# First attention of a two-part transformer block: plain F32 scores for both components in the two halves of the array, with seven weight chunks between the heads

## What is computed

```python
qkv = hn @ w_qkv                                  # hn: 512 x 1024, w_qkv: 1024 x 3072
q, k = apply_rope(q), apply_rope(k)               # (S, 8 heads, 2 components, 64)
s = einsum('bqhcd,bkhcd->bhcqk', q_blk, k) * scale
s = where(causal_mask, s, -inf)
p = softmax(s, axis=-1)
a = p[:, :, 0] - lam * p[:, :, 1]                 # the two components are combined
o = einsum('bhqk,bkhe->bqhe', a, v)
o = rms_norm(o, subln_g) * (1 - lambda_init)
h = h + o @ w_o
```

## Time and profile before

| what | value |
|---|---|
| median of 3 runs | 1865.9 us (1862.34 to 1867.95) |
| the profiled execution | 1863.19 us, with a span of 1861.4 us |
| PE busy | 1832.0 us, 98% of the span |
| DVE, ACT, POOL busy | 908.1, 614.0, 526.7 us |
| mean granted TensorE clock | 0.996 of full |

### The profile page before, as it was taken

The page is one execution under the profiler, slowest core; times in us unless marked ns, Lnnn a source line. Parts: engine busy times, 40 slices in busy tenths (PEclk is TensorE's granted clock), DMA queues, the critical chain, the costliest instruction groups (busy, mean ns, idle before and its releaser), DMA issues.

```text
span 1861.4 us, 22776 instructions
## 1 busy us (share of the span) xinstructions
PE 1832.0 (98%) x8694; PEld 1498.8 (81%) x8694; DVE 908.1 (49%) x1146; ACT 614.0 (33%) x888; POOL 526.7 (28%) x340
## 2 busy tenths in 40 slices
PE   9999999999999999999999999999999999999998
PEld 7897788888888876788888888777777888888876
DVE  7746753333335765453333335498655432333366
ACT  4236622122223335422222124233435232222352
POOL 1311355142325430153223245332112220210222
PEclk9999999999999999999999999999999999999999
DMA  5525322322322224225222222311112232232231
GB/s 181 163 91 117 101 93 95 106 93 90 107 96 90 91 98 136 93 90 125 100 104 90 95 105 91 121 68 68 46 60 94 89 109 90 90 113 91 90 113 68
DMA packets 40558, 183.94 MB, mean 99 GB/s; under 512 B 5512, under 2 KB 12200, under 8 KB 21416
## 3 DMA queue, kind: packets, MB, share of 16 engines
q1 hardware_dynamic: 38224, 179.26, 28.5%
q10 hardware_dynamic: 2264, 3.72, 1.0%
HBM read 161.99 MB, written 3.67 MB: 89 GB/s over the span
## 4 chain that ended last, share of the span: by engine, by line
PE 88%; DVE 6%; issue 2%; ACT 1%; POOL 1%; DMA 1%; SPq 0%; DVEq 0%; ACTq 0%; POOLq 0%
PE ps L496 23%; PE ps L497 23%; PE ps L498 23%; PE ps L546 4%; PE ps L535 4%; PE ps L536 4%; PE ps L705 1%; PE ps L896 1%; PE ps L914 1%; PE ps L819 1%; PE ps L809 1%; DVE probs L1612 1%; DVE wlo L1465 1%; DVE negmin L1591 1%; DVE idx_score L1879 1%
## 5 line engine op out<-in xcount | busy, mean ns | idle before, releaser
L1465 DVE TENSOR_TENSOR wlo<-raw,whi 128x2048 fp32r<-128x2048 f32 x138 | 341.7, 2476 | 325.8 <-ACT whi L1019 323.2
L1019 ACT ACTIVATE whi<-raw 128x2048 fp32r<-128x2048 f32 x147 | 280.6, 1909 | 373.0 <-PE ps L498 263.7
L496 PE MATMUL ps<-xb,whi 128*128 128x512 f32 x992 | 388.0, 391 | 3.2 <-ACT idx_relu L1294 1.3
L498 PE MATMUL ps<-xb,wlo 128*128 128x512 f32 x992 | 386.1, 389 | 0.0
L497 PE MATMUL ps<-xb,whi 128*128 128x512 f32 x992 | 386.0, 389 | 0.0
L496 PE MATMUL ps<-xa_hi,whi 128*128 128x512 f32 x788 | 307.6, 390 | 0.8 <-DVE wlo L1465 0.7
L498 PE MATMUL ps<-xa_hi,wlo 128*128 128x512 f32 x788 | 306.6, 389 | 0.0
L497 PE MATMUL ps<-xa_lo,whi 128*128 128x512 f32 x788 | 306.6, 389 | 0.0
L496 PEld LDWEIGHTS ps<-xb,whi 128*128 128x128 f32 x992 | 186.3, 188 | 44.1 <-issue 4.7
L498 PEld LDWEIGHTS ps<-xb,wlo 128*128 128x128 f32 x992 | 186.2, 188 | 39.2
L497 PEld LDWEIGHTS ps<-xb,whi 128*128 128x128 f32 x992 | 186.3, 188 | 38.2 <-issue 0.2
(11 more groups left out here) (324 smaller groups left out, 2524.0 us busy)
## 6 DMA issues: line engine op xcount, KB each, us to landing
raw<-wst SPq DMA_DIRECT2D x149, 1024.0 KB, 4.8
stage<-qk_split SPq DMA_DIRECT2D x64, 128.0 KB, 2.4
h<-xT ACTq DMA_DIRECT2D x4, 512.0 KB, 7.9
stage_k_lo<-qk_split SPq DMA_DIRECT2D x32, 64.0 KB, 2.0
mla_qn<-q_nope SPq DMA_DIRECT2D x8, 256.0 KB, 2.7
mla_v<-v_tok SPq DMA_DIRECT2D x8, 256.0 KB, 2.7
outT<-h SPq DMA_DIRECT2D x8, 256.0 KB, 2.0
bias_scratch<-bias_rows ACTq DMA_DIRECT2D x1, 1536.0 KB
```

What stands on the lines that cost most here:

```text
L496: pe.matmul(out, lhs_hi, rhs_hi, start=first, stop=False)
L498: return pe.matmul(out, lhs_lo, rhs_hi, start=False, stop=last)
L1019: act.activation(whi[slot][:, :], raw[slot][:, :], ACT.Copy).then_inc(whi_done, 1)
L1465: dve.tensor_tensor(wlo[slot][:, :], raw[slot][:, :], whi[slot][:, :].bitcast(F32), ALU.subtract).then_inc(wlo_done, 1)
```

## The change

The stages `qk`, `v` and `diff` become one stage `qkv` of 12 chunks in the order q, k, v for each pair of heads. Chunks 0 to 4 run ahead, and chunks 5 to 11 run one in each of the steps -1 to 5. The fp32r split of q and k is gone, with `qk_split`, `stage_k_lo` and the memsets that cleared its other half. `stage` now holds plain F32, component 0 in rows 0 to 63 and component 1 in rows 64 to 127, with 4 DMAs for each head. For each query block PE makes one F32 product over 64 rows for each component, one after the other into two banks, and then the two mask products. A single pair of banks takes the scores: banks 0 and 1 up to head 3 (`SWAP`), banks 2 and 3 from head 4, and for the last head the two pairs in turn. The other pair takes the chunk's tiles. The weighted sum of head n now stands in step n (before: n+1), and `turn` of head n-1 behind it (before: n-3). The loops over heads are written out.

```diff
-            def diff_scores(par, half, comp, first=False):
-                pe.wait_ge(stage_full[par][comp], 96 * (half + 1))
...
-                    pe.matmul(b[:, 0:wide], stage[par][:, comp, 0, q], stage[par][:, comp, 1, 0:wide], start=True, stop=False)
-                    pe.matmul(b[:, 0:wide], stage[par][:, comp, 0, q], stage_k_lo[par][comp][:, 0:wide],
-                              start=False, stop=False)
-                    mask_later(b[:, q]).then_inc(tile_done, 1)
+            def diff_scores(n, i):
+                banks = score_banks(n, i)
...
+                    for comp in range(2):
+                        pe.wait_ge(score_free[comp], 4 * n + i - (n == HEADS - 1 and i >= 2))
+                q = slice(P * i, P * i + P)
+                for comp in range(2):
+                    rows = slice(64 * comp, 64 * comp + 64)
+                    pe.matmul(ps[banks + comp][:, 0:P * (i + 1)], stage[n % 2][rows, 0, q],
+                              stage[n % 2][rows, 1, 0:P * (i + 1)], start=True, stop=False)
+                for comp in range(2):
+                    mask_later(ps[banks + comp][:, q]).then_inc(score_done, 1)
...
+            def diff_step(n):                      # PE
+                c = head_chunk(n)
+                if n == SWAP:
+                    diff_scores(n + 1, 0)
+                qkv_part(c, 0, (0, 1))
+                if n >= 0:
+                    diff_transposes(n, (0, 1, 2))
+                if n != SWAP:
+                    diff_scores(n + 1, 0)
+                if n >= 0:
+                    diff_transposes(n, (3,))
+                qkv_part(c, 1, (0,))
+                diff_scores(n + 1, 1)
+                qkv_part(c, 1, (1,))
+                diff_scores(n + 1, 2)
+                if n >= 0:
+                    diff_weighted(n)
+                diff_scores(n + 1, 3)
+                if n >= 1:
+                    turn(o_raw[(n - 1) % 2], n - 1, X["diff_o"] + n - 1)
...
+            for n in range(-1, HEADS - 2):
+                diff_step(n)
+            n = HEADS - 2
+            diff_scores(n + 1, 0)
+            diff_scores(n + 1, 1)
+            diff_transposes(n)
+            diff_scores(n + 1, 2)
+            diff_weighted(n)
+            diff_scores(n + 1, 3)
+            turn(o_raw[(n - 1) % 2], n - 1, X["diff_o"] + n - 1)
+            diff_transposes(n + 1)
+            diff_weighted(n + 1)
...
+            def diff_step(n):                      # DVE
+                c = head_chunk(n)
+                if n >= 0:
+                    diff_coefs(n)
+                    diff_combine(n)
+                if c is not None:
+                    lo(c + 1, (c + 1) % 2)
+                if n >= 2:
+                    head_lo(xb_lo, xb_hi, n - 2, X["diff_o"], gsub[:, 0:1])
+                if n >= 1:
+                    diff_mean_square(n - 1)
+                if is_rope(c):
+                    rope_part(c, 0)
+                if n < HEADS - 1:
+                    for i in range(3):
+                        diff_min(n + 1, i)
+                if is_rope(c):
+                    rope_part(c, 1)
+                if n < HEADS - 1:
+                    diff_min(n + 1, 3)
...
+            def diff_step(n):                      # ACT
+                c = head_chunk(n)
+                if n >= 2:
+                    head_hi(xb_hi, n - 2, 0, gsub[:, 0:1])
+                if c is not None:
+                    hi(c + 1, 0, 2 * c)
+                if n >= 0:
+                    copy_pT(pT, n % 2, n)
+                values = c is not None and not is_rope(c)
+                if values:
+                    take_v(c, 0)
+                diff_exp(n + 1, 0)
+                diff_exp(n + 1, 1)
+                if values:
+                    take_v(c, 1)
+                diff_exp(n + 1, 2)
+                if n >= 0:
+                    diff_copy_o(n % 2, n)
+                diff_exp(n + 1, 3)
...
             for dst, src in consts:                # SP
-            load_pairs(2, 6)
-            stage_diff(0, 0, True)
-            load_pairs(6, 8)
-            stage_diff(1, 0, True)
-            load_pairs(8, 14)
-            stage_late()
...
+            for c in range(2, 6):
+                load(c, c % 2)
+            stage_diff(0)
+            stage_diff(1)
+            for c in range(6, 9):
+                load(c, c % 2)
+            for n in range(2, 6):
+                stage_diff(n)
+                load(n + 7, (n + 7) % 2)
+            load(13, 1)
+            stage_diff(6)
+            stage_diff(7)
```

More of the change, by code:

```diff
@@ L80, with head_chunk, is_rope, score_banks @@
 STATS = [n if n < 7 else n - 1 for n in range(N_NORMS)]
+QKV_STEPS = range(5, 12)
+CHUNK_BANKS = (0, 2, 0, 2, 0, 2, 2, 2, 2, 0, 0, 0)
+CHUNK_USE = [CHUNK_BANKS[:c].count(CHUNK_BANKS[c]) for c in range(12)]
+SWAP = QKV_STEPS[CHUNK_BANKS[5:].index(0)] - 6
+def head_chunk(n):
+    return 6 + n if 6 + n in QKV_STEPS else None
+def is_rope(c):
+    return c is not None and c % 3 != 2
+def score_banks(n, i):
+    return (0 if n <= SWAP else 2) if n < HEADS - 1 or i % 2 == 0 else 0
 IDX_HEADS, TOPK = 8, 128
@@ L94 @@
 N_SILU = sum(GU_TILES)
-Q_LO, Q_HI, K_HI, K_LO = range(4)
 WARM = 18
@@ L399, in load_pairs, with stage_diff @@
                     load(c1 - 1, (c1 - 1) % 2)
-            def stage_diff(par, half, first):
-                if first:
-                    sp.wait_ge(split_lo, 4)
+            def stage_diff(n):
+                pair, par = n // 2, n % 2
+                sp.wait_ge(rope_done, 2 * pair + 2)
+                if pair:
+                    sp.wait_ge(score_done, 8 * (n - 1))
                 for comp in range(2):
-                    if not first:
-                        sp.wait_ge(tile_done, T["diff"] + 8 * par + 16 * half - 16 + 4 * (comp + 1))
                     for hf in range(2):
                         rows = slice(32 * (2 * par + comp), 32 * (2 * par + comp) + 32)
[L411 to L424, removed]
+                        sp.dma_start(stage[par][64 * comp + 32 * hf:64 * comp + 32 * hf + 32, :, :],
+                                     qk_raw[pair % 2][rows, hf, :, :]).then_inc(stage_full[par], 16)
             for part, full in ((FIRST, first_full), (SECOND, raw_full[0])):
@@ L667, in _ @@
                 pe.matmul(BC[:, 0:P], zeros[:, :], zeros[:, :], start=True, stop=True)
[L670 to L673, removed]
+            c = C["qkv"]
+            features(c % 2, c, T["qkv"], xa_hi, xa_lo, fresh=(xh_done, xl_done, X["qkv"]))
+            features((c + 1) % 2, c + 1, T["qkv"] + 2, xa_hi, xa_lo, hook=lambda k: late_rstd(0, k))
@@ L676, in mask_later @@
+            tokens(c % 2, c + 2, T["qkv"] + 4, xa_hi, xa_lo)
+            for u in (3, 4):
+                features((c + u) % 2, c + u, T["qkv"] + 2 * u, xa_hi, xa_lo)
             def mask_later(out):
                 return pe.matmul(out, ident_b[:, :], mask_b[:, :], start=False, stop=True)
[L680 to L694 removed]
@@ L699, in transposes @@
+            def transposes(src, ready, n, part=range(QT)):
+                for j in part:
+                    i = TR_ORDER[j]
                     pe.wait_ge(*ready(j, i))
@@ L727, in turn @@
                 mm.then_inc(ot_done, 1)
[L729 to L742, removed]
@@ L744, in _, with diff_transposes @@
-            pe.wait_ge(dve_const, 5)
[L745 to L754, removed]
+            def diff_transposes(n, part=range(QT)):
+                transposes(probs[n % 2][:, 0, :], lambda j, i: (a_done, 4 * n + j + 1), n, part)
@@ new lines, in diff_weighted @@
+            def diff_weighted(n):
+                if n % 2 == 0:
+                    c = 3 * (n // 2) + 2
+                    for u in range(2):
+                        pe.wait_ge(bank_free[CHUNK_BANKS[c] + u], CHUNK_USE[c] + 1)
+                weighted(pT[n % 2], v_tok, n, n, oc_done)
+            def diff_step(n):
[18 more added lines that the diff above has]
+                    turn(o_raw[(n - 1) % 2], n - 1, X["diff_o"] + n - 1)
@@ L1069, in _ @@
[L1069 to L1078, removed]
-                        tt = t + 2 * s + u
-                        act.wait_ge(tile_done, tt + 1 + 4 * i)
-                        for half in range(2):
-                            q = 2 * u + half
-                            ins = act.activation(v_tok[:, q, bass.ds(256 * s + 512 * i, 256)],
-                                                 ps[tt % 4][:, 256 * half:256 * half + 256],
-                                                 ACT.Copy, scale=rstd_t[:, q:q + 1])
-                        ins.then_inc(bank_free[tt % 4], 1)
@@ L1088, in _, with take_v @@
-            v_pair(0, first=True)
-            with act.Fori(1, 2) as i:
-                v_pair(i)
-            def diff_exp(par, half, comp):
-                n = 2 * half + par
-                for i in range(QT):
+            def take_v(c, u):
+                b = CHUNK_BANKS[c] + u
+                act.wait_ge(tile_done, 2 * c + u + 1)
+                for half in range(2):
```

(33 more changed lines are left out.)

215 lines of the change are left out of this document (95 added, 120 removed).

## The result

The changed kernel took 1868.11 us (median of 20 runs, 1866.56 to 1871.71) against 1863.38 for the kernel before on the same chip (20 runs, 1862.34 to 1867.95). The ratio is 1.0022, with a 95% interval of 1.0016 to 1.0028: the change costs 4 to 5 us, clear of the spread and less than 0.3%. Forecast were 1868 and +5.1.

What follows compares the result with a forecast made beforehand. PE, busy 98% of the span, was taken as the bound. Terms +2.1 + 0.5 - 9.2 + 11.0 + 1.4 - 0.7 gave +5.1 us on the profiled 1863.2, so 1868, range 1859 to 1878.

Steps and rivals of the forecast that it cites:

- scores, 8 heads: F32 score pairs with masks and edges on PE: 3.9 us a head against 3.64 before, +2.1 for eight heads.
- breaks: Cutting transposes and chunks around the scores costs PE about 0.1 us at five further places: +0.5.
- transposes: Ten transposes a head on PE, 1.52 us before; no saving on them was forecast.
- holes that go: PE's idle and slow stretches between dependent parts before the change, all counted as removed: -9.2 us.
- holes that come: New PE waits at step -1, step 3, the q and k steps, and steps 6 and 7: +11.0 us, bounds 6 to 17.
- slow clock: PE's clock drops once, after three holes of 2 to 3 us within 20 us: +1.4 us (0 to 4).
- load of chunk 7: Its load no longer queues on SP behind the first head's DMAs, so PE's idle goes: -0.7 us.
- halves that take turns (3): The two 64-row score products run in turn because each writes with a mask pending: +17 us, 1885; chance 0.05.
- second drain (2): A drain on both edges of each of 32 score pairs, 0.2 us more each: +6.4, 1875; chance 0.12.
- DVE did not become the bound (4): Rival claim: DVE bounds the q and k steps, 1.5 us late in four of them: +6, 1874; chance 0.13.
- Head 6's stage was in time (5): Rival claim: a stage or load arrives late at head 6 or behind `stage_diff`: +2 to +5 us, 1872; chance 0.06.
- Rival 1: The holes are covered after all, leaving PE's own work plus breaks: -7.3 us, 1856; chance 0.17.

Runs made afterwards that it cites:

- experiment 2: Changed kernel plus 32 extra F32 products that nothing reads, laid into its four longest holes; 1864.12 us, ratio 0.9999 to the kernel before.
- experiment 8: Changed kernel with all reorderings (start, end, early split, early minima): 1860.59 us, ratio 0.9982 to the kernel before; with 11 filler products added, 1860.12, 0.9975.
- experiment 1: Changed kernel with each component's full-array mask product directly behind its F32 product, between the two halves; 1898.03 us, ratio 1.0177 to the kernel before.

## Why the prediction was right

The forecast sum was +5.1. The medians differ by 4.7 and the spans by 3.6 (1865.0 and 1861.4); at the first product of `wo_a`, which is as far as the terms reach, the changed kernel is 4.1 behind. Term by term:

| term | forecast | trace after | how it is read |
|---|---|---|---|
| scores, 8 heads | +2.1 | +1.4 | a pair is 0.213(i+1) + 0.20 as forecast; two masks 0.12 and not 0.22: 3.45 a head; four entries into a pair at 0.09 (96.00 to 96.31): 3.8 |
| breaks | +0.5 | +1.8 | 20 resumptions of a chunk at 0.09 (104.49 to 104.81 is 0.32, where 0.23 is usual) |
| transposes | 0 | -2.5 | five of the eight groups are cut in two and take 1.03 without their entry (0.75 from 91.72, 0.37 from 93.01), not 1.52 |
| holes that go | -9.2 | -9.2 | the same subtraction, 71.4 less 62.2; PE was idle in 4.8 of it |
| holes that come | +11.0 | +9.0 | 1.95, 0.55, 0.28, 1.86, 1.56, 2.83; forecast 1.9, 0.5, 0.3, 2.1, 1.9, 3.8, and 0.5 |
| slow clock | +1.4 | +2.7 to +3.8 | products stretched by 1.5, 1.1 and 1.2 behind three holes |
| load of chunk 7 | -0.7 | -0.7 | no idle before that chunk |

The rows of the trace after add to +2.5 to +3.6, against +4.1, of which 0.3 lies ahead of 20 us (the first chunk starts at 20.36, before at 20.10); the rest I can't place. The transposes stood in no term of the forecast. They probably waited inside the group for the combination before, in part of the 1.52; that is not shown. The 1.1 of the stretched pairs at 202.73 lies ahead of another hole that ends with an exponential, so it was partly waited for anyway, as the filled hole of experiment 2 shows (2.0 and 2.1 long there instead of 1.86 and 1.56).

The main line held: F32 pairs run side by side and cost PE about what the split form did (3.8 a head, where 3.9 was forecast and 3.64 stood before), the holes inside the heads close, and the two ends of the stage, where no chunk is left to lay between, open again. The path of 2.5 us from a pair's end to its freed banks, and in step 4 the sum of DVE's work, predicted all six holes by place, five of them to 0.4 us and the last to 1.0. That the sum is close is partly luck: the scores came out 0.7 lower, the breaks 1.3 higher, the transposes, put at nothing, 2.5 lower, the holes 2.0 lower and the clock 1.3 to 2.4 higher. That 1868 was met to 0.1 us is luck too: the sum was put on the profiled execution (1863.2), and on the median then known it would have been 1871; over 20 runs the kernel before has 1863.38. The term most undersized for its weight was the clock: I counted one slow stretch, there were three, and experiment 2 puts them at about 4 us.

Of the rivals, halves that take turns (3) are out. A second drain (2) is there at under half its price: all 32 entries into a pair cost about 0.09, 2.9 us in all where the rival had 6.4, and the forecast counted two of the four entries in a head. DVE did not become the bound (4): its only late minimum cost 0.28. Head 6's stage was in time (5). Rival 1, that the holes are covered, did not happen by itself; experiment 8 shows that over half of their length can go.

## What to carry to other kernels

Price a cheaper or merged product by what must come back before the next one can start, not only by its own time: the same pairs cost 14 us with four banks and nothing between them, and 4 in the new order, with chunk products between. When work is spread between dependent parts, look first at the steps at both ends that get none, and move the next stage's products there together with the splits and copies that they will wait for. Where PE must wait some 2 us all the same, try filling the wait with a few products that nothing reads: here that held the clock at 1.00 and alone was worth about 4 us (experiment 2).

## What the runs showed of the hardware

Products over rows 0 to 63 and 64 to 127 overlap fully when one follows the other directly, and no longer when a full-array mask stands between them (1.15 against 2.31 us for a 512-wide pair with masks). A group of 64-row products costs about 0.20 beyond its columns, and about 0.09 more on the product ahead of it. The 0.20 is the same for one product (109.79 to 110.85 in experiment 1) as for a pair (103.34 to 104.40 after). The Trainium skill (TensorEngine Tiling (Array Packing), Key Properties) says that changing the tiling mode drains the engine. The trace agrees in that there is a fixed cost at the change; that it is a drain no run here shows.

The price of a hole is not fixed by its length. The hole of 1.95 us was followed by 3.49 at a granted clock of 0.54, the one of 0.55 by none, and the one of 1.56 ahead of 208.50 by none either:

```profile
208.50:212.00 3.50, 3.50 (x28) 2.83 (x30) 1.02 (x2) 2.05 (x9) 0.25 (x1) 1.00 0.02 5
```

Nor is it fixed by the program. In the second profile of the changed kernel the hole of 1.86 came at the same place, and the pair behind it took 0.43 and not the 0.70 of the first (202.73 to 203.43); there the hole ahead of the third block had the slow clock behind it:

```profile
202.74 0.49 PE L707 MATMUL ps<-stage 64*128 64x128 f32 x4 [1.86 <-ACT probs L1142]
203.17 0.29 PE L684 MATMUL ps<-mask_b,ident_b 128*128 128x128 bf16 x2
...
207.76 1.65 PE L707 MATMUL ps<-stage 64*128 64x384 f32 x4 [1.48 <-ACT probs L1142]
```

The two profiles differ in the same way far behind the change; these are windows of the first and of the second:

```profile
1400.00:1450.00 50.00, 47.47 (x210) 38.32 (x209) 27.47 (x32) 26.45 (x39) 11.74 (x9) 0.97 0.28 102
```

```profile
1400.00:1450.00 50.00, 47.17 (x202) 38.23 (x201) 26.33 (x31) 26.42 (x39) 11.69 (x9) 0.93 0.31 106
```

With a window from 200 to 232 us that went from 0.89 to 0.84 too, this is most of the 3.9 us between their spans (1865.0 and 1868.9). For a change of 0.2% one trace is not enough to place a microsecond, and the reading of the slow clock in the table above is that of one execution.
